# Keys chosen beside the even projection's jobs, output turned in the next projection, and four feed-forwards that compute rows of tokens

## The reference

```python
def swiglu(x, wg, wu, wd):                       # wg, wu: 1024 x 2816, wd: 2816 x 1024
    return (jax.nn.silu(x @ wg) * (x @ wu)) @ wd
...
# even_mixer
aq, ak, av, iq, ik, iw, bq, bk, bv = jnp.split(h @ w_in, cuts, axis=-1)
out_a = dsa_attention(aq, ak, av, iq, ik, iw, t5_bias[:, :8])
lam = exp(sum(lq1 * lk1)) - exp(sum(lq2 * lk2)) + lambda_init
out_b = diff_attention(bq, bk, bv, lam, b_subln, t5_bias[:, 8:]) * (1.0 - lambda_init)
return jnp.concatenate([out_a, out_b], axis=-1) @ w_out
...
# dsa_attention: the keys that a query may use
idx_logits = jnp.einsum('bqhd,bsd->bqhs', iqb, ik) * 64 ** -0.5
score = jnp.einsum('bqh,bqhs->bqs', iwb, jax.nn.relu(idx_logits))
_, sel = lax.top_k(score, 64)
```

## Time and profile before

| | |
|---|---|
| timed runs, median of 3 (lowest, highest) | 1747.04 us (1746.64, 1747.14) |
| profiled execution: own time, span | 1735.48 us, 1733.9 us |
| busy: PE, PEld, DVE, ACT | 1653.0, 1486.4, 1066.8, 853.1 us |
| mean granted clock | 0.969 |
| 128x256 matmuls with weights stationary, high and low | 5640 |
| weight slots | 257, 1 MB each, 4.8 us from issue to landing |
| projection of the even mixer | about 708 to 796.55 us |
| its `Lambda` and `Select` | to 814 us |
| its attention | 814.67 to 866.03 us |

### The profile page before, as it was taken

One profiled execution on the slowest core, in us unless ns is written; L12 is line 12 of the kernel. 1 busy time (PEld: TensorE's weight loads), 2 busy tenths in 40 slices (PEclk: granted clock), 3 DMA queues, 4 the chain that ended last, 5 costly groups with the idle time before them and its releaser, 6 DMA issues.

```text
span 1733.9 us, 25053 instructions
## 1 busy us (share of the span) xinstructions
PE 1653.0 (95%) x10412; PEld 1486.4 (86%) x10412; DVE 1066.8 (62%) x1545; ACT 853.1 (49%) x1223; POOL 23.6 (1%) x26
## 2 busy tenths in 40 slices
PE   7988988999999999997989999999999999999998
PEld 7876877899989998885777999889998878789997
DVE  5555658688756564676757665455554766766553
ACT  4454645666545443553446544354443555664442
POOL 0000002000000000000000000000000000000000
PEclk9988989999999999997689999999999999999999
DMA  7747223555554555442033554545554542525553
GB/s 272 275 146 245 101 98 146 190 187 180 187 191 163 179 190 193 177 172 95 1 131 137 194 189 176 194 173 191 173 192 170 194 146 74 190 102 187 178 194 122
DMA packets 42976, 290.21 MB, mean 167 GB/s; under 512 B 5048, under 2 KB 5198, under 8 KB 9968
## 3 DMA queue, kind: packets, MB, share of 16 engines
q1 hardware_dynamic: 38272, 271.93, 43.8%
q0 software_dynamic: 4592, 16.69, 2.8%
HBM read 287.51 MB, written 8.55 MB: 171 GB/s over the span
## 4 chain that ended last, share of the span: by engine, by line
PE 88%; DVE 5%; DMA 2%; ACT 2%; issue 1%; DVEq 1%; SPq 0%; POOL 0%; ACTq 0%
PE bank L454 26%; PE bank L455 26%; PE bank L456 26%; PE bank L460 7%; DMA raw<-stream_dram 2%; PE bank L724 2%; DVE low L422 1%; PE bank L1504 1%; PE bank L606 1%; DVEq L2414 1%; ACT high L411 1%; PE bank L1702 0%; DVE u L983 0%; DVE h L1109 0%; DVE u L659 0%
## 5 line engine op out<-in xcount | busy, mean ns | idle before, releaser
L411 ACT ACTIVATE high<-raw 128x2048 fp32r<-128x2048 f32 x257 | 488.9, 1914 | 535.4 <-DMA raw<-stream_dram 525.7
L422 DVE TENSOR_TENSOR low<-raw,high 128x2048 fp32r<-128x2048 f32 x255 | 582.8, 2293 | 248.1 <-ACT high L411 246.9
L454 PE MATMUL bank<-xh,high 128*128 128x256 f32 x1880 | 535.1, 285 | 1.1 <-DVE low L422 1.1
L455 PE MATMUL bank<-xl,high 128*128 128x256 f32 x1880 | 533.5, 284 | 0.0
L456 PE MATMUL bank<-xh,low 128*128 128x256 f32 x1880 | 533.5, 284 | 0.0
L454 PEld LDWEIGHTS bank<-xh,high 128*128 128x128 f32 x1880 | 362.3, 193 | 2.1 <-issue 1.5
L455 PEld LDWEIGHTS bank<-xl,high 128*128 128x128 f32 x1880 | 362.3, 193 | 0.0
L456 PEld LDWEIGHTS bank<-xh,low 128*128 128x128 f32 x1880 | 362.2, 193 | 0.0
L454 PE MATMUL bank<-high,xh 128*128 128x512 f32 (+2 forms) x528 | 206.7, 391 | 5.6 <-DVEq L2414 3.2
L456 PE MATMUL bank<-high,xl 128*128 128x512 f32 (+2 forms) x528 | 203.6, 386 | 0.0
L455 PE MATMUL bank<-low,xh 128*128 128x512 f32 (+2 forms) x528 | 203.5, 385 | 0.0
(11 more groups left out here) (229 smaller groups left out, 1555.9 us busy)
## 6 DMA issues: line engine op xcount, KB each, us to landing
raw<-stream_dram SPq DMA_DIRECT2D x257, 1024.0 KB, 4.8
band_wide_dram<-band_rows_dram POOLq DMA_DIRECT2D x1, 3072.0 KB, 30.9
t_wide_dram<-t_rows_dram POOLq DMA_DIRECT2D x1, 2304.0 KB, 15.1
u<-mem_dram POOLq DMA_DIRECT2D x2, 1024.0 KB, 5.2
bias<-band_wide_dram POOLq DMA_DIRECT2D x1, 2048.0 KB, 15.3
rel_wide_dram<-rel_rows_dram POOLq DMA_DIRECT2D x1, 1920.0 KB, 15.7
bias<-t_wide_dram POOLq DMA_DIRECT2D x1, 1536.0 KB, 8.2
bias<-rel_wide_dram POOLq DMA_DIRECT2D x1, 1280.0 KB, 7.0
```

The lines of the kernel that those rows point to most:

```text
L411: act.activation(self.high[:, n % RING, :], self.raw[:, n % RING, :], ACT.Copy).then_inc(self.high_split, 1)
L422: dve.tensor_tensor(self.low[:, n % RING, :], self.raw[:, n % RING, :], self.high[:, n % RING, :].bitcast(F32), ALU.subtract).then_inc(sel ...
L454: pe.matmul(out, lh, rh, start=start, stop=False)
L455: pe.matmul(out, lh, rl, start=False, stop=False)
```

## The change

1. The four feed-forwards of the layers become `RowFfn`. Eleven chunks of 512 moving columns (256 of gate, 256 of value) are computed with the tokens stationary, for both token blocks; two slots a chunk. Silu takes its factor per row. The product of chunk c-1 is turned by four 128x128 turnings behind the fourth weight tile of chunk c (the last one behind the first tile of the down side) and then split to `hh`/`hl`. The down side waits for `hidden_ready` of the tenth chunk first. `Ffn` of the first block stays.
2. `Lambda` and `Select` are no stages any more. `Select` is called from `Project`: scores behind tiles 2 and 5 of jobs 3 to 6 (block 1 first), relu on ScalarE and sums on VectorE ahead of that job's draining, searches in jobs 4 to 7, lambda in job 6. Job 1 is now the index queries. The turning ring is two banks instead of four, since scores take banks 6 and 7.
3. `Attention` runs no searches and gets `fill=16`.
4. The `out_turn` stage goes. `TurnedResidual` turns `dsa_attention`'s half at once, and norms and turns the other half behind the first weight tile of `even_out`.

```diff
-    main = r(0, 512) + r(512, 512) + r(1536, 512) + r(2120, 512) + r(2632, 512) + r(1024, 512) + r(3144, 512)
+    main = r(1536, 512) + r(0, 512) + r(512, 512) + r(2120, 512) + r(2632, 512) + r(1024, 512) + r(3144, 512)
...
-        plan += [(f"up1_{layer}", FT * 2 * KT, P), (f"down1_{layer}", 2 * FT, HALF)]
+        plan += [(f"up1_{layer}", FT * KT // 2, HALF), (f"down1_{layer}", 2 * FT, HALF)]
...
+    def sides(g, u):
+        g, u = by_chunk(g, S), by_chunk(u, S)
+        return [np.concatenate(two, 1) for two in zip(g, u)]
...
-            pieces[f"up{n}_{layer}"] = pairs(g(f"ffn{n}_wg"), g(f"ffn{n}_wu"))
+            pieces[f"up{n}_{layer}"] = sides(g(f"ffn{n}_wg"), g(f"ffn{n}_wu"))
...
-    def __init__(self, core, batches, base=0):
+    def __init__(self, core, batches, base=0, ring=4):
         super().__init__(core)
-        self.base, self.batches = base, []
+        self.base, self.ring, self.batches = base, ring, []
...
                     c.release(last, m, i0 + j)
+                if self.select:
+                    self.select.tensor(pe, s, n, j)
...
             c.split_high(act, m.slot(i0 + len(kts) - 1))
+            if self.select:
+                self.select.scalar(act, s, n)
...
             c.split_low(dve, m.slot(i0 + len(kts) - 1))
+            if self.select:
+                self.select.vector(dve, s, step, n)
...
+class TurnedResidual(Residual):
+    def __init__(self, core, name, x, kts, turn, **options):
+        super().__init__(core, name, x, kts, **options)
+        self.turn = turn
+    def input_wait(self, pe, s, k):
+        if k == 0:
+            self.turn.turn_rows(pe, s, 0)
+        pe.wait_ge(s["turned_by_dve"], NB if k < self.kts // 2 else 2 * NB)
+        if k == 1:
+            self.turn.turn_rows(pe, s, 1)
+    def scalar(self, act, s):
+        self.turn.copy_high(act, s, 0)
+        self.turn.square_rows(act, s, 1)
+        self.core.split_high(act, self.m.first)
+        self.turn.copy_high(act, s, 1)
+        super().scalar(act, s)
+    def vector(self, dve, s):
+        self.turn.copy_low(dve, s, 0)
+        self.turn.scale_rows(dve, s, 1, Steps(dve, s["dve_step"]))
+        self.core.split_low(dve, self.m.first)
+        self.turn.copy_low(dve, s, 1)
+        super().vector(dve, s)
...
         Residual.vector(self, dve, s)
+class RowFfn(Ffn):
+    CHUNKS = FT // 2
+    def __init__(self, core, up, down, source, factor=1.0, **options):
+        super().__init__(core, up, down, source, factor, **options)
+        work = core.square[:, :, :].rearrange("p a b -> p (a b)")
+        part = lambda at: work[:, at:at + 2 * HALF].rearrange("p (n b w) -> p n b w", n=2, b=NB)
+        self.gate_rows, self.product_rows = part(0), part(2 * HALF)
+    def sums(self, c, b):
+        return self.core.bank[2 * (c % 2) + b]
+    def turned(self, c):
+        return self.core.bank[4 + c % 2 if c < self.CHUNKS - 1 else 2][:, :]
+    def turn_chunk(self, pe, s, c):
+        pe.wait_ge(s["gates_ready"], 2 * c + 2)
+        if c >= 2:
+            pe.wait_ge(s["hidden_ready"], c - 1)
+        for j in range(2):
+            for b in range(NB):
+                at = j * S + b * P
+                last = pe.transpose(self.turned(c)[:, at:at + P], self.product_rows[:, c % 2, b, j * P:(j + 1) * P],
+                                    self.core.ident)
+        last.then_inc(s["tiles_turned"], 1)
+    def tensor(self, pe, s):
+        core = self.core
+        self.rows.begin(pe, s)
+        for c in range(self.CHUNKS):
+            if c >= 2:
+                pe.wait_ge(s["gates_ready"], 2 * c - 2)
+            for k in range(KT):
+                if c == 0:
+                    self.rows.arrive(pe, s, k)
+                    self.rows.next(pe, s, k)
+                i = c * KT + k
+                w = core.piece(pe, self.up, i)
+                for b in range(NB):
+                    last = mm3(pe, self.sums(c, b)[:, :], (core.xh[:, k, block_cut(b)], core.xl[:, k, block_cut(b)]), w,
+                               k == 0, k == KT - 1)
+                    if k == KT - 1 and b == 0:
+                        last.then_inc(s["banks_filled"], 1)
+                core.release(last, self.up, i)
+                if k == KT // 2 - 1 and c:
+                    self.turn_chunk(pe, s, c - 1)
+        pe.wait_ge(s["hidden_ready"], self.CHUNKS - 1)
+        Residual.tensor(self, pe, s)
+    def input_wait(self, pe, s, k):
+        if k == 1:
+            self.turn_chunk(pe, s, self.CHUNKS - 1)
+        pe.wait_ge(s["hidden_ready"], k // 2 + 1)
+    def scalar(self, act, s):
+        core = self.core
+        self.rows.scalar(act, s)
+        core.split_high(act, self.up.first)
+        act.wait_ge(s["inverse_ready"], 1)
+        for c in range(self.CHUNKS + 1):
+            core.split_high(act, self.up.first + 2 * c + (1 if c < self.CHUNKS else 0))
+            if c:
+                act.wait_ge(s["tiles_turned"], c)
+                act.activation(core.hh[:, 2 * c - 2:2 * c, :].rearrange("p n q -> p (n q)"), self.turned(c - 1), ACT.Copy)\
+                   .then_inc(s["highs_ready"], 1)
+            if c < self.CHUNKS:
+                for b in range(NB):
+                    if b:
+                        act.wait_ge(core.slot_used, self.up.slot(c * KT + KT - 1) + 1)
+                    else:
+                        act.wait_ge(s["banks_filled"], c + 1)
+                        if c >= 2:
+                            act.wait_ge(s["gates_ready"], 2 * c - 2)
+                    act.activation(self.gate_rows[:, c % 2, b, :], self.sums(c, b)[:, 0:S], ACT.Silu,
+                                   scale=core.inv[:, 2 + b:3 + b]).then_inc(s["inputs_ready"], 1)
+        Residual.scalar(self, act, s)
+    def vector(self, dve, s):
+        core = self.core
+        self.rows.lows(dve, s)
+        core.split_low(dve, self.up.first + 1 - LEAD)
+        self.rows.vector_norms(dve, s, self.factor)
+        core.split_low(dve, self.up.first)
+        for c in range(self.CHUNKS + 1):
+            core.split_low(dve, self.up.first + 2 * c + (1 if c < self.CHUNKS else 0))
+            if c:
+                dve.wait_ge(s["highs_ready"], c)
+                cut = (slice(None), slice(2 * c - 2, 2 * c))
+                dve.tensor_tensor(core.hl[cut].rearrange("p n q -> p (n q)"), self.turned(c - 1),
+                                  core.hh[cut].rearrange("p n q -> p (n q)").bitcast(F32), ALU.subtract)\
+                   .then_inc(s["hidden_ready"], 1)
+            if c < self.CHUNKS:
+                for b in range(NB):
+                    dve.wait_ge(s["inputs_ready"], 2 * c + b + 1)
+                    if c >= 2:
+                        dve.wait_ge(s["tiles_turned"], c - 1)
+                    dve.tensor_tensor(self.product_rows[:, c % 2, b, :], self.gate_rows[:, c % 2, b, :],
+                                      self.sums(c, b)[:, S:HALF], ALU.mult).then_inc(s["gates_ready"], 1)
+        Residual.vector(self, dve, s)
...
-class Select(Stage):
+class Select:
+    FIRST = 3
+    UNITS = [(b, pair) for b in (1, 0) for pair in ((0, 2), (1, 3), (4, 6), (5, 7))]
+    TILES = (2, 5)
+    PARTS = {4: (4,), 5: (5,), 6: (6, 7), 7: (0, 1, 2, 3)}
+    LAMBDA = 6
...
+    def of_job(self, n):
+        first = 2 * (n - self.FIRST)
+        return [i for i in (first, first + 1) if 0 <= i < len(self.UNITS)]
+    def tensor(self, pe, s, n, k):
+        if not self.of_job(n) or k not in self.TILES:
+            return
+        c = self.core
+        i = self.of_job(n)[self.TILES.index(k)]
+        b, pair = self.UNITS[i]
+        nk = (b + 1) * P
+        if i == 0:
+            pe.wait_ge(s["turned_by_act"], 2)
+            pe.wait_ge(s["turned_by_dve"], 2)
+        if i >= 2:
+            pe.wait_ge(s["keys_positive"], i - 1)
+        for j, h in enumerate(pair):
+            last = mm(pe, c.bank[6 + i % 2][:, j * S:j * S + nk], self.q(h)[:, b * P:(b + 1) * P],
+                      self.k(h)[:, 0:nk], True, True)
+        last.then_inc(s["keys_scored"], 1)
+    def scalar(self, act, s, n):
+        c = self.core
+        for i in self.of_job(n):
...
+            b, pair = self.UNITS[i]
             nk = (b + 1) * P
+            act.wait_ge(s["keys_scored"], i + 1)
             if i >= 2:
-                pe.wait_ge(s["probs_ready"], i - 1)
+                act.wait_ge(s["keys_summed"], i - 1)
+            ps = c.bank[6 + i % 2][:, :].rearrange("p (j k) -> p j k", j=2)[:, :, 0:nk]
+            act.activation(self.positive(i)[:, :, 0:nk], ps, ACT.Relu, scale=DH ** -0.5)\
+               .then_inc(s["keys_positive"], 1)
+        if n == self.LAMBDA:
+            act.wait_ge(s["lam_sums"], 1)
+            act.activation(c.small[:, 146:148], c.small[:, 144:146], ACT.Exp).then_inc(s["lam_exps"], 1)
+    def vector(self, dve, s, step, n):
+        if n == self.FIRST:
+            for b in range(NB):
+                step(dve.tensor_scalar(self.w[:, b, :], self.weights(b), 8 ** -0.5, None, ALU.mult))
```

(51 more changed lines are left out.)

97 lines of the change are left out of this document (27 added, 70 removed).

## The result

The changed kernel took 1702.69 us (median of four runs, 1700.71 to 1705.0) beside 1746.84 of the kernel before: ratio 0.9754, 95% interval 0.9732 to 0.9775. I had forecast 1715.3, range 1706 to 1730. Its profiled execution took 1705.0 (span 1703.2), that of before 1735.48. Between these two the difference is 30.5, and I had worked out 31.7.

The account below looks back on a forecast made before the run. TensorE, busy 95% of the span, was taken as the bound. Terms -9.6+14.0-17.8-11.0-7.3 gave -31.7 us, so 1703.8 from the profiled 1735.48; with 11.6 added for timed runs, 1715.3, range 1706 to 1730.

Parts of the forecast that it names:

- the last one: Transfer from profile to timed runs: 11.6 us added to the profiled sum of 1703.8, giving 1715.3.
- Feed-forwards: Four feed-forwards: wider matmuls save 7.0 us each, eleven groups of turnings at 0.44 add 4.8; 9.6 less in all.
- The waits: Feed-forwards: TensorE's waits for chunk c-1 and the tenth chunk stay hidden, with 2.4 and 1.35 us to spare.
- (b): Feed-forwards: turnings cost 0.6 us more a group and the tenth chunk is late, 0.6 per feed-forward: 1725; chance 0.09.
- (d): Feed-forwards: 44 groups of turnings break the matmul stream; slower than before from 1.16 us a group; chance 0.04.
- (e): Feed-forwards: no gain from width, a matmul of 512 costs 240 ns, as two of 256: 1743; chance 0.03.
- Projection and the two stages: Even mixer: choosing keys inside the projection makes it 14.0 us longer; dropping the lambda and key-choice stages saves 17.8.
- Attention: Even attention: filling restores 2.4 GHz and searches leave, 40.4 us against 51.4, so -11.0; bounds -14 and +1.
- Output: Attention's output turned inside the next projection: 7.3 us less; 5.3 if norms came late, 8.2 if turnings were free.
- Rival (a): Even attention: the clock stays low despite the filling, about 14 us more: 1729; chance 0.14.
- Rival (c): Projection: VectorE keeps up, TensorE idles under 3 us and the clock holds: 1709; chance 0.06.

Follow-up runs that it names:

- before_fourth: The kernel before, unchanged, profiled for the fourth time: own time 1747.50 us, even mixer 203.1.
- after_again: The changed kernel, unchanged, timed and profiled again: median 1704.54 us (0.9786), profile 1706.94.
- twice_turned: The changed kernel with each group of four turnings in the four feed-forwards made twice, one profiled execution: the four stages grew by 4.6, 4.6, 5.1 and 4.6 us.
- six_ahead: The changed kernel with six tiles instead of four turned at once in the feed-forward whose tiles aren't turned early: 1703.3 us (0.9773).
- turn_apart: The changed kernel with its output turned in a stage of its own, as before: 1713.65 us (0.9831).
- old_ffn: The changed kernel with its four feed-forwards as before: median 1716.17 us (0.9848), first profile 1708.52.
- old_ffn_third: Third profile of the changed kernel with its four feed-forwards as before: 1718.70 us, even mixer 173.4.
- no_fill: The changed kernel without the sixteen filling matmuls of the even attention: 1717.64 us (0.9862).
- rows_only: The kernel before with only the four feed-forwards changed: 1726.02 us (0.9902).
- before_again: The kernel before, unchanged, profiled and timed again: profile 1739.60 us, median of 12 timed runs 1741.52.
- search_late: The changed kernel with the search of the first block's keys moved from job 7 of the projection into the attention, behind units 2 to 5: 1707.78 us (0.9798).

## Why the prediction was wrong

The step that failed is the last one: "The timed runs lie 11.6 above it with a spread of 0.5, and I apply the difference to their median." This takes the 11.6 us for something that both kernels carry. Most of it was the very thing that the change removes: the rest of the attention at half clock. Between the first profiled execution of before and before_fourth, which has the time of those timed runs, lie 12.0 us, and 10.2 of them are in the even mixer (8.0 between first score and last output); 1.9 are in the first mixer, which the change doesn't touch. With before_fourth in place of the first, the even mixer gives 203.1-168.1 = 35.0 and the feed-forwards 7.0, together 42.0. The first mixer differs by 0.6 more, which makes the 42.5 between before_fourth and the profiled execution of the changed kernel. The rest of the 44.2 measured is that the timed median of the changed kernel lies 2.3 below its own profiled execution and before_fourth 0.7 above its median.

The 44.2 itself depends on which executions of before stand beside it. In the group of after_again the same two kernels lie 38.8 apart (1743.3 and 1704.54), which is what an even mixer of 200.2 gives: 200.2-168.1+7.0 = 39.1. The forecast of 31.7 less is too small against either.

That the edited stages of the two profiled executions also give 31.7 is in part luck: the feed-forwards gave 2.6 less than forecast and the projection 0.4 less, the attention 2.9 more and the output 0.1 more.

The terms by themselves, profile against profile:

- **Feed-forwards**, 9.6 predicted, 7.0 measured. The pace was right: from 1051.79 to 1061.31 are 42 matmuls of 0.2267 us. The group of turnings was mis-sized, at 0.44. From one group to the next are 11.36 us, and 48 matmuls of 0.2267 are 10.88, so a group costs 0.48. The first matmul behind it takes 0.31 to the start of the second, and the few after that are slightly slow as well. Eleven groups of 0.48 give 7.0-5.3+0.2 = 1.9 us less for a feed-forward, as three of the four measure (1.9, 1.9, 2.0). In twice_turned groups are 11.78 apart: four more turnings in the same group cost 0.42, four in a break of their own 0.48.

```profile
1049.95 0.60 PE L1338 MATMUL bank<-const,square 128*128 128x128 f32 x4
...
1051.79 0.39 PE L459 MATMUL bank<-high,xh 128*128 128x512 f32 x1
...
1061.31 0.60 PE L1338 MATMUL bank<-const,square 128*128 128x128 f32 x4
1061.67 0.48 PE L459 MATMUL bank<-high,xh 128*128 128x512 f32 x1
1061.98 0.40 PE L460 MATMUL bank<-low,xh 128*128 128x512 f32 x1
```

  The first of the four gave only 1.2, 0.75 less than the others, which I had not seen. Four of its tiles are turned one by one inside the first chunk, ScalarE takes up the norms and the next split only behind the last of them, and the second slot's split is late. The row below shows this wait; it adds 0.5 us (1.21 from the start before it instead of 0.68). six_ahead turned six at once, the wait was gone and the stage 1.1 shorter. So it is shown that the late turnings cost this much; how the other 0.6 splits is not.

```profile
532.36 0.50 PE L459 MATMUL bank<-high,xh 128*128 128x512 f32 x1 [0.37 <-DVE low L427]
```

- **The waits** of chunk c-1 and of the tenth chunk cost nothing: neither shows as idle time.
- **Rivals (b), (d) and (e)** asked for a group of 0.6 or 1.16 us or more, or for 240 ns a matmul of 512; measured are 0.48 and 226.7. The Trainium skill, "TensorE: Matmul & The Clock Gate", Part 4: PE-mode transpose, has about 275 ns for one transpose in a kernel; twice_turned gives 105 here. The Trainium skill's same page, Back-to-back issue gap, gives N/2.4 + 2.5 ns for an isolated matmul, by which 512 columns are 215.8 ns (an estimate from that formula); the stream here has 226.7.
- **Projection and the two stages**, +14.0-17.8 = -3.8 predicted. From the mixer's start to the first score it was 106.5 before (708.15 to 814.67) and is 103.1 after (708.28 to 811.35): -3.4. From job 3's first matmul at 737.58, VectorE's evictions of jobs 4 to 7 start at 29.9, 43.6, 60.9 and 72.8; I had 29.2, 42.9, 60.1 and 72.4. TensorE ended at 67.8 and not 66.0, so it was idle for 6.0 and not 7. The list of VectorE's work in order was the most exact part of the working.
- **Attention**, -11.0 predicted, 37.5 us instead of 51.4 (811.35 to 848.87): -13.9. The first turning came after 4.9 us (I had 5.4), what follows took 32.65 (I had 35.0). That is full overlap by my own figures, 17.9+15.2 = 33.1; with the 5.4 in front they make -12.9, so the bound of -14 was not their sum. The part from 850.5 to 866.03, which I took at 15.2, is 15.5. I let TensorE and VectorE alternate for half of it; in the window above TensorE is busy for 30.48 of 32.67.
- **Output**, -7.3: from 34.97 (866.03 to 901.0) to 27.53, -7.4. turn_apart gives 6.8 from the other side; there the output's first matmuls run at full clock, and the forecast had 1.2 for those of before at half clock.
- **Rival (a)**, 0.14: the clock stays low. It did not in any of the seven profiles of kernels with the even mixer as changed (after, after_again, old_ffn three times, six_ahead, twice_turned). Its price was right: without the filling the mixer takes 13.7 more. Rival (c) was wrong too, since VectorE is late; that its 1709 lies nearer to the result is chance.

What I should have asked is where 11.6 us can be between executions of one kernel. The profile shows little that can vary from run to run, and the earlier trace rows show the largest: a clock that is at 0.50 for 33 us of dense work and then returns for no cause that the rows give. An execution in which it returns late is dearer by about half of the attention's rest. None of the seven profiles of the changed mixer has this; one of them, old_ffn_third, lost the clock again before the attention's end, and its mixer was 5 us longer.

What stays open: why the clock came back at 836, 839 and 851 us in three executions (no_fill, rows_only, before), and only behind the attention in the other three of before, at 880, 883 and 892, with the same or nearly the same work. Open too is why the first mixer takes 321 us in one execution and 327 in another, which would make up the spread of the changed kernel. Its granted clock goes with its length: over the first 320 us it is 0.95 in the two executions with 321.5 and 321.6, and 0.92 in the longest, 326.9 (windows of old_ffn, then of after_again). So the clock probably has a part in this as well; no run here tests it.

```profile
0.00:320.00 320.00, 282.21 (x1600) 243.53 (x1601) 192.76 (x336) 165.37 (x275) 15.99 (x16) 0.95 0.50 182
```
```profile
0.00:320.00 320.00, 283.04 (x1569) 244.85 (x1570) 187.51 (x328) 162.48 (x270) 16.02 (x16) 0.92 0.50 180
```

Of the timed runs only time and mean clock are known, so that their even mixers take 200 to 203 is worked out from four profiles, not seen in each. rows_only has one profile; that its other three runs (1725.9 to 1726.5) had the clock back in mid-attention follows from their times alone. Its four runs, with the feed-forwards' 7.0 added back, come to 1731.0 to 1733.5, and only three of the 64 runs of before (the 52 and before_again's 12) are as low as that or lower. So the shift is hardly chance, but why shorter feed-forwards bring the clock back sooner is not shown.

## What to carry to other kernels

When the profiled execution and the timed runs of a kernel differ by more than their spread, find the stage in which they can differ before a difference is carried over: an edit that touches this stage gains or loses the excess as well. Compare stage by stage, from one fixed instruction to the next: here nearly all stages but the two mixers repeat within 0.1 us, so that one profile measures an edit of 1 us that the timed runs can't resolve. Work moved off a busy engine is worth its length only if the clock survives the gap that it leaves; search_late freed 5.0 us and gave 8.1 back. Of these some 5.6 came behind 839 us, where its clock fell (838.93 to the mixer's end takes 39.4 us, and 33.8 from the same instruction of the changed kernel); the other 2.5 came before it, in the stretch with the searches.

## What the runs showed of the hardware

- TensorE stayed at 1.2 GHz through 59 us of attention in which it was busy for over 95% (before_fourth, 57.8 of 60.4 us, 0.50 in both windows above). It came back 4 us after the first score where sixteen filling matmuls followed the scores (0.59 over 4.85 us in the changed kernel, so half clock for 4.0 of them, then 1.00).
- An edit outside the mixer went with a change of this: with nothing but shorter feed-forwards, the same mixer took 188.9 us in the one profile of rows_only, and 192.9, 200.3, 200.2 and 203.1 in the four of before.
- A matmul of 512 columns with the tokens stationary has the same pace of 226.7 ns in the feed-forwards (42 in a row) as in the projection. A group of four turnings between such matmuls costs 0.48 us, and four more in the same group (twice_turned) 0.42.
